# One pass of the input projection's weights for two tiles, and the gates' offset as a matrix product

## What is computed

```python
def first_block(x, ...):
    xn = rms_norm(h, ln1_g[layer])
    proj = xn @ w_in[layer]                       # (512, 1024) @ (1024, 4096)
    u_s5, q, k, v, gate_logits = jnp.split(proj, splits, axis=-1)   # 512, 1024, 256, 256, 2048
    gates = jax.nn.sigmoid(gate_logits + b_gate[layer])
    g_s5, g_attn = jnp.split(gates, 2, axis=-1)
    y_s5 = s5_mixer(u_s5, ...) @ w_s5_branch[layer]
    y_attn = sliding_window_attention(q, k, v, ...) @ w_attn_branch[layer]
    h = h + (g_s5 * y_s5 + g_attn * y_attn) @ w_out[layer]
    xn2 = rms_norm(h, ln2_g[layer])
    h = h + peer_mixer(xn2, ...)                  # 8 heads x 16 experts of 16384 for each token
```

## Time and profile before

| | us |
|---|---|
| three runs | 3434.38, 3434.86, 3447.71 |
| median | 3434.86 |
| the profiled execution, whole | 3428.02 |
| its span in the profile | 3426.5 |

### The profile page before, as it was taken

How to read it: one execution, slowest core, us unless ns; L and a number is a source line. 1 busy time by engine, 2 the same in 40 slices (tenths; PEclk the granted TensorE clock), 3 DMA queues, 4 the chain that set the end, 5 groups by cost and what they waited for, 6 DMA issues and landing times.

```text
span 3426.5 us, 40200 instructions
## 1 busy us (share of the span) xinstructions
PE 2462.4 (72%) x13672; PEld 962.9 (28%) x13672; DVE 2380.6 (69%) x5690; ACT 1368.1 (40%) x3646; POOL 1122.9 (33%) x1038
## 2 busy tenths in 40 slices
PE   7668679667696777876677767767677768865555
PEld 3423333223332233322222223222232223311111
DVE  7438884687845969478664986668775987667764
ACT  1213442334423443343373436533383437533332
POOL 0001442223422244332333324332333334334442
PEclk9688889988897987988778888889898889987777
DMA  7669999999999999999999999999999999999997
GB/s 247 210 219 367 405 411 410 416 393 411 409 404 416 416 411 407 410 417 404 396 419 413 414 392 409 418 417 413 399 419 416 413 402 419 417 418 409 420 418 328
DMA packets 229599, 1349.38 MB, mean 394 GB/s; under 512 B 28537, under 2 KB 33945, under 8 KB 97554
## 3 DMA queue, kind: packets, MB, share of 16 engines
q0 software_dynamic: 148320, 1076.50, 77.0%
q1 hardware_dynamic: 80400, 268.20, 20.4%
q10 hardware_dynamic: 674, 2.13, 0.2%
HBM read 1344.01 MB, written 2.72 MB: 393 GB/s over the span
## 4 chain that ended last, share of the span: by engine, by line
DMA 31%; PE 25%; DVE 18%; issue 15%; POOL 6%; ACT 4%; POOLq 0%; ACTq 0%; DVEq 0%
DMA ring<-in_k_uv,idx 13%; PE ps L1550 12%; DMA ring<-in_k_vu,idx 10%; PE ps L1479 8%; DMA wsl<-in_k_wu 8%; DVE ring L378 7%; POOL ring L1956 6%; DVE big L426 2%; ACT L1132 1%; PE ps L1532 1%; PE ps L1693 1%; DVE rowB L426 1%; PE ps L1639 1%; ACT diag L1132 1%; ACT xr L1132 1%
## 5 line engine op out<-in xcount | busy, mean ns | idle before, releaser
L378 DVE CUSTOM_DVE_ANT_0 ring<-ring,xn 128x1024 f32<-128x1024 f32 x1024 | 1239.5, 1220 | 498.6 <-DMA ring<-in_k_vu,idx 258.3
L1479 PE MATMUL ps<-ring,diag 64*64 64x512 f32 x8192 | 1243.1, 727 | 422.1 <-ACT diag L1132 384.4
L1956 POOL DMA_INDIRECT ring<-in_k_vu,idx x514 | 558.7, 1087 | 1157.5 <-DVE aw L378 805.3
L1956 POOL DMA_INDIRECT ring<-in_k_uv,idx x510 | 558.1, 1094 | 1048.1 <-DVE aw L378 789.0
L1550 PE MATMUL ps<-wsl,xT 128*128 128x512 f32 (+1 forms) x1536 | 734.5, 623 | 106.3 <-DMA wsl<-in_k_wu 84.7
L1479 PEld LDWEIGHTS ps<-ring,diag 64*64 64x64 f32 x8192 | 301.1, 155 | 1129.4 <-ACT diag L1132 627.1
L1132 ACT ACTIVATE aw<-aw 128x2 f32<-128x2 f32 x512 | 103.8, 203 | 1185.6 <-DVE aw L378 1184.1
L1132 ACT ACT_TABLE_LOAD x373 | 478.6, 1283 | 66.7 <-DVE big L426 52.9
L1550 PEld LDWEIGHTS ps<-wsl,xT 128*128 128x128 f32 x1536 | 290.8, 200 | 557.8 <-issue 414.4
L1132 ACT ACTIVATE diag<-gid,aw 128x64 f32<-128x64 f32 x1024 | 306.8, 341 | 139.8 <-PE ps L1479 123.4
L1132 ACT ACTIVATE gid<-ident,gate 128x64 f32<-128x64 f32 x1024 | 292.5, 333 | 0.0
(11 more groups left out here) (230 smaller groups left out, 2040.4 us busy)
## 6 DMA issues: line engine op xcount, KB each, us to landing
wsl<-in_k_wu SPq DMA_DIRECT2D x408, 512.0 KB, 12.2
wsl<-in_k_wmod SPq DMA_DIRECT2D x48, 512.0 KB, 17.1
ring<-in_k_vu,idx POOLq DMA_INDIRECT x514
ring<-in_k_uv,idx POOLq DMA_INDIRECT x510
wsl<-in_k_wu SPq DMA_DIRECT2D x16, 280.0 KB, 15.9
big<-in_b_gate SPq DMA_DIRECT2D x4, 1024.0 KB, 11.4
big<-in_conv_w SPq DMA_DIRECT2D x4, 768.0 KB, 28.3
big<-modd SPq DMA_DIRECT2D x5, 512.0 KB, 11.8
```

Of the source, the lines that this page charges most:

```text
L378: V(v.tensor_tensor_reduce(u_row(s), u_row(s), xn[:, b, :], 1.0, 0.0, ALU.mult, ALU.add, aw[:, b, k:k + 1]), ("dot", s))
L1479: r = t.matmul(PA[half][64 * q:64 * q + 64, :], diag[64 * half:64 * half + 64, s % (2 * PAIR), :], v_row(s)[64 * half:64 * half + 64, 512 ...
L1956: Q(p.indirect_dma_start(out=both_rows(s), out_offset=None, in_=tab, in_offset=bass.IndirectOffsetOnAxis(ap=idx[:, n % 2, k:k + 1], axis=0 ...
```

## The change

Tile 2's norm is moved to the start of tile 1 (`norm_ahead`): the turned tile goes to `xT2`, which is a buffer of `xn` that is free by then. `project` for tile 1 multiplies every unit twice, with `xT` and with `xT2`, the second into PSUM banks 2 and 3. ScalarE copies tile 2's blocks out into two halves of `sq` (with the sigmoid for blocks 4 to 7), and each is written to DRAM (`w2d`, 256 KB for each block, 2.1 MB in all) by a DMA that ScalarE issues; the block two later waits for that DMA to land. In tile 1's `qk` ScalarE waits for the last two writes before it uses `sq` again. Tile 2 has no `norm` and no projection of its own: its 32 units are gone from `units`, and SyncE loads the blocks back with five DMAs ahead of tile 2's first remaining unit, behind a wait that stood there before (`mod_e` 7: the last column block of tile 1's `mods` is done).

For all four tiles, `b_gate` is loaded as one row of 8 KB in place of 1 MB, and enters each gate block as a matmul of a row of 128 ones by 512 elements of it, ahead of the block's eight. VectorE's addition (`gate_logits`) is gone, and ScalarE takes the sigmoid from PSUM.

Two new tables share out the slots: tile 1 has `norm` 5, `win` 40, `qk` 6, `mid` 44, `branch` 11, `route` 9, `top` 13 in place of 4, 25, 7, 52, 14, 11, 15; tile 2 has 1, 34, 7, 50, 13, 10, 13. So tile 1's `win` now reaches slot 33, `mid` runs from slot 39 to 83, `branch` to `top` from 83 to 116; tile 2's `win` to slot 151, `mid` from 158 to 208, the rest to 244.

```diff
@@ -24,6 +24,8 @@
+L1A_PARTS = (("norm", 5), ("win", 40), ("qk", 6), ("mid", 44), ("branch", 11), ("route", 9), ("top", 13))
+L1B_PARTS = (("norm", 1), ("win", 34), ("qk", 7), ("mid", 50), ("branch", 13), ("route", 10), ("top", 13))
@@ -167,6 +170,7 @@
+        w2d = nc.dram_tensor("aheadd", [128, 4096], F32, kind="Internal").ap()
@@ -207,6 +211,7 @@
+        xT2 = xn[:, 1, :].rearrange("p (a b) -> p a b", b=128)
@@ -304,16 +309,16 @@
-        units = [(n,) + u for n in range(8) for u in weight_units(n // 4)]
+        units = [(n,) + u for n in range(8) for u in weight_units(n // 4) if (n, u[0]) != (2, "win")]
...
-        for n, before in enumerate(((0, "glu"), (2, "win"), (3, "win"))):
+        for n, before in enumerate(((0, "glu"), (2, "glu"), (3, "win"))):
...
-            parts = L1_PARTS if n < 4 else L2_PARTS
+            parts = {1: L1A_PARTS, 2: L1B_PARTS}.get(n, L1_PARTS if n < 4 else L2_PARTS)
@@ -535,12 +541,15 @@
-            def gate_logits(n, b):
-                g_ = gt[:, 512 * (b - 4):512 * (b - 3)]
-                V.stage("win")
-                V.wait_ge("win", n, b)
-                V.wait_ge("gt", n)
-                V(tt(g_, PS[4 + b % 2], g_, ALU.add), ("gl", n, b))
+            def norm_ahead():
+                V.stage("norm")
+                rstd(2, "n", 5, D)
+                V(ts(xr[:, :], hres[:, 2, :], st[:, 5:6], None, ALU.mult, None), ("xr", 2))
+                for hh in range(2):
+                    V.wait_ge("xr_t", 2, hh)
+                    V(tt(xT2[:, 4 * hh:4 * hh + 4, :], P3(hh), bc(g1c[:, 4 * hh:4 * hh + 4].unsqueeze(2), [128, 4, 128]),
+                         ALU.mult), ("xT", 2, hh))
@@ -1232,6 +1238,22 @@
+            def norm_ahead():
+                S.stage("norm")
+                S.wait_ge("x", 2)
+                S.wait_ge("xr_t", 1, 1)
+                rstd(2, "n", 5, hres[:, 2, :], xr[:, :])
+            def ahead(b):
+                half = sq[:, 512 * (b % 2):512 * (b % 2) + 512]
+                S.wait_ge("win", 2, b)
+                if b >= 2:
+                    S.wait_ge("ahead_d", b - 2)
+                S(act(half, PS[2 + b % 2], ACT.Copy if b < 4 else ACT.Sigmoid), ("wea", b))
+                S.wait_own()
+                Q(a.dma_start(w2d[:, 512 * b:512 * b + 512], half), "ahead_d%d" % (b % 2), ("ahead_d", b))
             def gates(n, h):
@@ -1245,10 +1267,14 @@
+                    if n == 2:
+                        continue
...
+                        if n == 1:
+                            S.wait_ge("xr_t", 2, 1)
@@ -1259,13 +1285,20 @@
                         g_ = gt[:, 512 * (b - 4):512 * (b - 3)]
-                        S.wait_ge("gl", n, b)
-                        S(act(g_, g_, ACT.Sigmoid), ("gs", n, b))
+                        S(act(g_, p, ACT.Sigmoid), ("gs", n, b))
+                    if n == 1:
+                        ahead(b)
...
                 S.wait_ge("we", n, 3)
+                if n == 2:
+                    S.wait_ge("ahead_q")
+                    S.wait_ge("ahead_k")
+                if n == 1:
+                    S.wait_ge("ahead_d", 6)
+                    S.wait_ge("ahead_d", 7)
                 S(act(sq, qs, ACT.Square), ("qsq", n))
@@ -1544,12 +1580,29 @@
                     if u == 0 and b >= 2:
-                        T.wait_ge(*(("gl", n, b - 2) if n < 4 and b >= 6 else ("we", n, b - 2)))
+                        T.wait_ge(*(("gs", n, b - 2) if n < 4 and b >= 6 else ("we", n, b - 2)))
+                    offset = name == "win" and n < 4 and b >= 4
+                    if offset and u == 0:
+                        T.wait_ge("ones")
+                        T.wait_ge("gt", n)
+                        t.matmul(PS[bank], ones[0:1, :], gt[0:1, 512 * (b - 4):512 * (b - 3)], start=True, stop=False)
                     for j in range(2):
...
                         r = t.matmul(PS[bank][:, 0:nn], lhsT(kk_), wsl[:, at % NWS, j, 0:nn],
-                                     start=(kk_ == 0), stop=(kk_ == nk - 1))
-                    T(r, ("unit_used", at), *([(name, n, b)] if 2 * u + 2 == nk else []))
+                                     start=(kk_ == 0 and not offset), stop=(kk_ == nk - 1))
+                    done = [(name, n, b)] if 2 * u + 2 == nk else []
+                    if ahead:
+                        if u == 0 and b >= 2:
+                            T.wait_ge("wea", b - 2)
+                        if offset and u == 0:
+                            t.matmul(PS[bank - 2], ones[0:1, :], gt[0:1, 512 * (b - 4):512 * (b - 3)], start=True,
+                                     stop=False)
+                        for j in range(2):
+                            kk_ = 2 * u + j
+                            r = t.matmul(PS[bank - 2][:, 0:nn], xT2[:, kk_, :], wsl[:, at % NWS, j, 0:nn],
+                                         start=(kk_ == 0 and not offset), stop=(kk_ == nk - 1))
+                        done += [(name, n + 1, b)] if 2 * u + 2 == nk else []
+                    T(r, ("unit_used", at), *done)
                     if 2 * u + 2 == nk and b in after:
@@ -1598,6 +1658,9 @@
                     T.wait_ge("yT", 0, 2)
+                if n == 1:
+                    T.wait_ge("wea", 6)
+                    T.wait_ge("wea", 7)
                 turn([kk[:, 0:128], kk[:, 128:256]], 2, ("kT_t", n))
@@ -1894,16 +1957,22 @@
             for n in range(4):
-                norm(n)
+                if n != 2:
+                    norm(n)
+                if n == 1:
+                    norm_ahead()
                 if n == 0:
...
                     make_bias(1, 8)
-                if n:
+                if n == 1:
+                    project(1, "win", xk, "win", 0.0, 1.0, ("xT", 1, 0), ("xT", 1, 1), ("q_e", 0, 1), ("xT", 2, 0),
+                            ("xT", 2, 1), ahead=True)
+                elif n == 3:
                     project(n, "win", xk, "win", 0.0, 1.0, ("xT", n, 0), ("xT", n, 1), ("q_e", n - 1, 1))
-                else:
+                elif n == 0:
                     project(0, "win", xk, "win", 0.0, 1.0, ("xT", 0, 0), ("xT", 0, 1),
@@ -1994,11 +2063,21 @@
                     load(bmod, A["k_bmod"][:, n, :, :], "bmod", n)
+                if (n, name, b, u) == (2, "glu", 0, 0):
+                    Y.wait_ge("h", 1, 1)
+                    Y.wait_ge("ahead_d", 6)
+                    Y.wait_ge("ahead_d", 7)
+                    Y.wait_ge("q_t", 1, 1)
+                    Q(s.dma_start(xr[:, 0:512], w2d[:, 0:512]), "ahead_u", ("we", 2, 0))
+                    load(qs, w2d[:, 512:1536], "ahead_q")
+                    load(kk, w2d[:, 1536:1792], "ahead_k")
+                    Q(s.dma_start(v1[:, 0, :], w2d[:, 1792:2048]), "ahead_v", ("we", 2, 3))
+                    Q(s.dma_start(gt, w2d[:, 2048:4096]), "ahead_g", *[("gs", 2, b) for b in range(4, 8)])
                 if n < 4 and (name, b, u) == ("win", 3 if n == 0 else 2, 0):
...
                         Y.wait_ge("h", n - 1, 1)
-                    Q(s.dma_start(gt, A["b_gate"][0].unsqueeze(0).broadcast_to([128, 2048])), "gt", ("gt", n))
-                if (n, name, b, u) == (2, "win", 4, 0):
+                    Q(s.dma_start(gt[0:1, :], A["b_gate"]), "gt", ("gt", n))
+                if (n, name, b, u) == (2, "attb", 0, 0):
                     for q in range(4):
```

30 lines of the change are left out of this document (19 added, 11 removed).

## The result

The changed kernel takes 3443.4 us (median of 20 runs) against 3433.5 us for the kernel before (20 runs): a ratio of 1.0030, 95% interval 1.0022 to 1.0038. It is slower by 10 us, where 17 us less were forecast. The difference is real but lies inside the 0.5% that I called no change. The profiled execution took 3438.7 us, its span 3437.3. One of the twelve executions of one variant (e10) took 7379 us, a slow run, and is left out of its median.

What follows compares the result with a forecast made beforehand. Bounds by stage: DMA in `branch` to `top`, VectorE in `mid`, TensorE in the new pass. Tile 1 +26.5, tile 2 -33.9, tiles 0 and 3 -9.5: -17 us, 3411 profiled, 3418 median, range 3388 to 3448.

Steps and rivals of the forecast that it cites:

- tile 0: Tile 0 as a whole: -7 us (-10 to 0), from -5 behind TensorE's end and -2 for that end itself.
- the two credits: Tile 1's `branch` to `top`: -5 us for a fuller ring, -5 us for six units of tile 2 no longer loaded.
- norm ahead: Tile 2's norm standing before tile 1's projection: +5.3 us (4 to 8).
- pass of tile 1: Tile 1's `win` with both tiles' matmuls: TensorE sets the end, 148 us against 92.4, +55.6 us.
- `qk` of tile 1: ScalarE's wait for the last two writes, taken as 5 us to land: +3.8 us (0 to 11).
- `mid` of tile 1: 44 slots for 52 at VectorE's pace of 1.15 us each: -9.2 us, so 126.4.
- `branch` to `top`, tile 1: 33 slots for 42 at 2.52 us each, plus credits: 134 us against 163.0, -29 us (-33 to -14).
- `win` of tile 2: Without matmuls, VectorE's heads and dots 96 us, then waits for fetches: 102 us against 120.0, -18 us.
- The chain of 5 us behind the end: Tile 0's `qk`: with VectorE's gate addition gone, the first sum follows TensorE's end sooner, -5 us.
- Rival 2: TensorE's clock stays low in the long pass: at 0.83 it takes 175 us, whole +10, 3445 us; chance 0.15.
- Rival 3: Stages behind don't give back: tile 1's `branch` to `top` 149 us, write 12 us, whole 3440 us; chance 0.15.
- Rival 1: The DMA is the bound throughout: 16.8 MB saved at 416 GB/s, whole -50, 3385 us; chance 0.20 with its half-way.

Runs made afterwards that it cites:

- e10: Kernel before with blocks 0 to 3 of tile 2 shared, products of ones, and 36 and 30 slots for 30 and 28 in the projections; 3426.8 us, ratio 0.9986.
- e7: The changed kernel with the slot tables of before for tiles 1 and 2; 3456.6 us, ratio 1.0067 to the kernel before.
- e4: The changed kernel with the last two written blocks in fin, so the squares of q wait only for earlier writes; 3439.9 us, ratio 1.0022 to the kernel before.
- e6: The changed kernel with 45 slots for 40 in the pass and 39 for 34 in tile 2's projection; 3446.8 us, ratio 1.0045 to the kernel before.
- e1: The kernel before with the gates' offset as products of ones in all four tiles and nothing shared; 3420.4 us, ratio 0.9966.

## Why the prediction was wrong

Three steps failed by the most: the end of TensorE's work in tile 0, forecast 2 us earlier and measured 6 us later; the two credits in `branch` to `top` of tile 1, with the price of a slot there; and the VectorE time of tile 2's `win`. The bound that I named for the pass, TensorE, was right.

| step | forecast | first profile |
|---|---|---|
| tile 0 | -7 | +3.5 |
| norm ahead | +5.3 | +5.5 |
| pass of tile 1 | 148 | 150.8 |
| `qk` of tile 1 | 21.7 | 23.9 |
| `mid` of tile 1 | 126.4 | 126.5 |
| `branch` to `top`, tile 1 | 134 | 141.1 |
| `win` of tile 2 | 102 | 106.8 |
| `qk` and `mid` of tile 2 | 154 | 150.5 |
| `branch` to `top`, tile 2 | 151 | 154.1 |
| tile 3 (measured: all behind tile 2) | -2.5 | -2.2 |

The forecast for the profiled execution was 3411 and it took 3438.7: 28 us, to which the rows of the table add up.

- **Tile 0 failed, 10 us.** The step said "TensorE's end itself moves by -1 MB (the gate rows, at the DMA's pace) and +3.5 us of ones: -2". Its own terms don't give -2: 1 MB at the transfer's pace is -2.5, and with +3.5 that is +1. The end moved by +6 in the first profile and by 6 to 9 in twelve profiles with the products against four without. The load of the 1 MB was issued at 29.6 us in the kernel before, 60 us ahead of the last projections, so it was not what they waited for. The chain of 5 us behind the end was right. With both parts the step would have been about +1; what is left of the +3.5 is of the size by which tile 0's middle stage differs between executions, with the clock.
- **`branch` to `top` of tile 1 failed in size, 7 us.** Nine slots were priced at 2.52 us each; seven slots between e7 and the changed kernel gave 2.1 each, so 4 us of the 7 are the price. The other 3 are the two credits of 5 us: I had booked 6 of the 10 (134 us, not 130), and 3 came. The stage moved 56.9 MB for 67.3 before, 10.4 less, of which nine slots are 9.4: a fuller ring and six unloaded units together were worth 1 MB, 2 us. A ring that `mid` fills was nothing new: VectorE waited for rows in `mid` for 0.8 us before, and not at all after the change.
- **`win` of tile 2 failed in size, 5 us.** Most of it lies in VectorE's part, and not in the fetches behind it. By the forecast's own prices the heads end 84.6 us into the stage (six heads, 25 dot products, 1 us); they end after 88.7, with 26 dot products, 2.6 us of waits, and 9.4 us for a head between slots (753.1 to 767.1, with four dot products) where I had 9.13. The end was nearly as forecast: five fetched rows had landed, and the next four slots waited for theirs: 18 us from the heads' end to `qk`, for my 17. The dot products at the heads' end, five in a row and then the first that waits (timeline, VectorE):

```profile
797.92 1.22 DVE L383 CUSTOM_DVE_ANT_0 ring<-ring,xn 128x1024 f32<-128x1024 f32 x1
...
802.50 1.22 DVE L383 CUSTOM_DVE_ANT_0 ring<-ring,xn 128x1024 f32<-128x1024 f32 x1
...
805.89 1.23 DVE L383 CUSTOM_DVE_ANT_0 ring<-ring,xn 128x1024 f32<-128x1024 f32 x1 [2.17 <-DMA ring<-in_k_uv,idx]
```

- **The pass, 3 us.** Its bound and its clock were right. A product of ones took 1.06 us from its start to the next for my 0.87 (eight: 1.5 us more), and three slots more fell into it than the 27 that I had counted (236 to 240 records of their matmuls, eight for a slot).
- **`qk` of tile 1, 2 us.** The writes landed after 8.3 us (median) for my 5; the trace shows the wait as 5.4 us, and e4 takes it away.

The rivals. Rival 2, the low clock, did not happen: the pass ran at 0.99, near 2.4 GHz, though it went through four PSUM banks with 512 columns each. The page "TensorE: Matmul & The Clock Gate" of the Trainium skill (section "A second HAM failure mode: psum-queue depth-cycling") tells of a bf16 kernel whose engine idles in bits between its groups of matmuls, so that the clock swings between two levels. This trace has the four banks and not the idle bits, TensorE being busy for 150.8 of 150.8 us, and the clock did not swing. Rival 3 named nearly the right time, 3440, by a floor of 149 us; the stage took 141 us, and 140 in e6 with five slots less, so the floor lies near there. Its other half, the slow write, is the part that was true. Rival 1 had the right account, bytes, and forgot the other side of it, idle.

The deeper error is that the sum was made stage by stage with the old stages' slack taken as given. Two steps on different resources were compared as differences to the time before, and nowhere did I ask how long the DMA engines would stand still in all. That question needs one line: at 410 GB/s the new kernel's bytes take 800 us, so any time under 859 had to come from less than 59 us of idle transfer. The pass alone, at my own 148 us and 51 MB, has 23 of them, where the kernel before had 12 in two tiles. I also summed both halves of the change into one number, and so did not see that one half, e1's, could bring a gain and the other a loss.

## What to carry to other kernels

Where nearly every stage runs at the transfer's rate, a saving of bytes is worth what it says only if it doesn't make another engine the bound somewhere: book saved bytes against the new idle time of the DMA engines, stage by stage, before anything else. Work that is merged into one pass lands on the engine that the merged stage has least of; here TensorE was 84% busy in that stage (89% in e1, with the products of ones) before it got twice the matmuls, and even half of them more was too much. And split a change that has two ideas: the products of ones alone are 0.34% faster than the kernel before, and their median is below that of every kernel with sharing that keeps the computation whole.

## What the runs showed of the hardware

- A product with a single row on the contracting side takes 1.06 us for 512 columns of float32 from its start to the next (332.67 to 333.73 in the pass), more than a full one's 0.86 in a row of them. So leaving out 127 of the 128 rows saves nothing. The 0.2 us on top is near the 0.17 us that the earlier trace rows show for a change of kind; whether it is that was not tested.
- A write of 256 KB to DRAM took 8.3 us in the median from issue to landing, while the DMA engines were 90% busy. The page "DMA: Bandwidth & Descriptors" of the Trainium skill (section "Anatomy of one DMA — SWDGE (gpsimd) path") gives, for DMAs of GpSimd's path, 2.0 us plus the bytes at 436 GB/s, an estimate of 2.6 us for this size. This write was issued by ScalarE, and the measurement decides; whether the busy queue or the path makes the difference was not tested.
- TensorE's granted clock in the middle stage of tile 0 came out between 0.54 and 0.72 in 16 profiles of nearly the same instructions. At 0.54 the next stage started at 160.5 to 162.5 us, at 0.72 at 154.7 and 155.7.
